# Expert 31's up product in two halves around expert 30's turning products, ahead of its down product

## The reference

```
y = lax.map(expert_block, (x_rows, block_expert))      # per block: its rows, its expert
def expert_block(args):
    xb, e = args
    return (jax.nn.silu(xb @ w1[e]) * (xb @ w3[e])) @ w2[e]
out = jnp.zeros((N, C), F32).at[row_tok].add(y.astype(F32) * row_gate[:, None])
```

## Time and profile before

| | us |
|---|---|
| median of 3 runs | 2261.11 |
| lowest and highest of them | 2261.01, 2263.4 |
| span of the profiled execution, from its first instruction to its last | 2258.9 |
| what lies between that span and the median | 2.2 |
| experts of the first layer in the trace | about 706 to 1199 |
| experts of the second layer in the trace | about 1740 to 2227 |

### The profile page before, as it was taken

How to read it: one execution, slowest core, us unless ns; L and a number is a source line. 1 busy time by engine, 2 the same in 40 slices (tenths; PEclk the granted TensorE clock), 3 DMA queues, 4 the chain that set the end, 5 groups by cost and what they waited for, 6 DMA issues and landing times.

```text
span 2258.9 us, 34449 instructions
## 1 busy us (share of the span) xinstructions
PE 1941.9 (86%) x14540; PEld 1055.0 (47%) x14540; DVE 863.9 (38%) x1608; ACT 454.8 (20%) x1103; POOL 193.1 (9%) x234
## 2 busy tenths in 40 slices
PE   6999788899997888787876999999998888887773
PEld 5843787756744333233333445546845333333321
DVE  6655766674463111101113565761465111110113
ACT  2042666411211000000002005611112000000001
POOL 1000221110001111111110000000000111111110
PEclk9999999999998999999998999999998999999997
DMA  4310001312248999999993222024245999999995
GB/s 151 100 50 0 13 5 61 113 47 102 78 195 309 411 409 405 407 403 415 406 410 134 75 75 75 8 87 149 78 186 222 401 412 408 413 412 409 405 410 199
DMA packets 92146, 510.90 MB, mean 226 GB/s; under 512 B 21824, under 2 KB 22984, under 8 KB 67184
## 3 DMA queue, kind: packets, MB, share of 16 engines
q1 hardware_dynamic: 80896, 492.15, 55.6%
q0 software_dynamic: 10880, 16.81, 2.2%
q10 hardware_dynamic: 240, 0.07, 0.0%
HBM read 503.73 MB, written 24.12 MB: 234 GB/s over the span
## 4 chain that ended last, share of the span: by engine, by line
PE 69%; DMA 17%; DVE 8%; ACT 3%; issue 3%; SPq 0%; ACTq 0%; POOLq 0%; DVEq 0%
DMA big<-in_moe_w 16%; PE ps L2607 15%; PE ps L2063 13%; PE ps L2059 9%; PE ps L2638 7%; PE ps L2042 2%; PE ps L2140 2%; PE ps L2255 2%; PE ps L2408 1%; PE ps L2506 1%; PE ps L2188 1%; PE ps L2518 1%; PE ps L2029 1%; PE ps L2369 1%; PE ps L2414 1%
## 5 line engine op out<-in xcount | busy, mean ns | idle before, releaser
L2607 PE MATMUL ps<-big 128*64 128x512 f32 x2048 | 467.2, 610 | 40.3 <-DMA big<-in_moe_w 37.1
L2607 PEld LDWEIGHTS ps<-big 128*64 128x64 f32 x2048 | 155.9, 140 | 301.6 <-issue 290.5
L2063 PE MATMUL ps<-big 128*128 128x512 f32 x672 | 289.7, 592 | 0.0
L2638 PE MATMUL ps<-big 128*64 128x512 f32 x1024 | 255.9, 646 | 32.6 <-ACT big L1177 32.6
L1916 DVE SCALAR_TENSOR_TENSOR big<-big,ps 128x256 f32<-128x256 f32 x64 | 27.0, 421 | 487.8 <-ACT big L1170 487.8
L2059 PE MATMUL ps<-big 128*128 128x256 f32 x896 | 196.5, 382 | 6.3 <-DVE big L1400 6.3
L2063 PEld LDWEIGHTS ps<-big 128*128 128x128 f32 x672 | 127.4, 190 | 159.0 <-issue 158.7
L1907 DVE TENSOR_TENSOR big<-ps,gain_ffn 128x512 f32<-128x512 f32 x66 | 45.6, 691 | 373.1 <-PE ps L2644 373.1
L2059 PEld LDWEIGHTS ps<-big 128*128 128x128 f32 x896 | 171.8, 192 | 30.3 <-issue 6.5
L2638 PEld LDWEIGHTS ps<-big 128*64 128x64 f32 x1024 | 73.8, 146 | 167.1 <-issue 139.8
L1170 ACT ACTIVATE big<-ps 128x256 f32<-128x256 f32 x64 | 24.6, 384 | 533.1 <-PE ps L2607 533.1
(11 more groups left out here) (351 smaller groups left out, 2442.6 us busy)
## 6 DMA issues: line engine op xcount, KB each, us to landing
big<-in_moe_w SPq DMA_DIRECT2D x182, 2048.0 KB, 31.6
big<-in_rw_wrkv SPq DMA_DIRECT2D x12, 1024.0 KB, 5.1
big<-in_mx_wkv SPq DMA_DIRECT2D x12, 1024.0 KB, 5.0
big<-in_moe_w SPq DMA_DIRECT2D x12, 1024.0 KB, 35.7
big<-in_mb_wqkv SPq DMA_DIRECT2D x12, 1024.0 KB, 6.6
big<-in_mx_wq SPq DMA_DIRECT2D x8, 1024.0 KB, 6.4
big<-in_mx_wo SPq DMA_DIRECT2D x8, 1024.0 KB, 5.0
big<-in_moe_w SPq DMA_DIRECT2D x16, 512.0 KB, 6.9
```

The lines of the kernel that those rows point to most:

```text
L2063: ins = mm(d[:], lhsT=acts[:, k, i * P:(i + 1) * P], rhs=quarter(w)[:, k], start=k == 0, stop=k == 3)
L2607: ins = mm(ps[2 + b][half * BR:(half + 1) * BR, :], lhsT=hgT[b][:, k], rhs=w13[set_][:, :, k, half * 256:(half + 1) * 256], start=k == 0, ...
L2638: ins = mm(ps[5 + b][half * BR:(half + 1) * BR, :], lhsT=hT[b][:, f * BR:(f + 1) * BR], rhs=w2[set_][:, f, half * HB:(half + 1) * HB], sta ...
```

## The change

The last expert's `up` (block 31) is cut into two halves by k. In the step of block 30, PE now does the first half of `up` 31, `turn_act` 30, the second half of `up` 31, `rows_in` for block 32, and `down` 30. The wait for the gathered rows of block 32, which stood in the middle of `down`, is also made ahead of `rows_in`. The diff:

```
 def up(b, set_, number, turn, ks):

+    last = isinstance(number, int) and number == E - 1
     if 0 in ks:
         pe.wait_ge(rowsT_out[l], number + 1)
         pe.wait_ge(act_ready[l], number - 1 + PRE)
-        last = isinstance(number, int) and number == E - 1
...
     ahead = (1 - b, set_1, number + 1, turn_1)
+    if isinstance(number, int) and number in (E - 3, E - 2):
+        up(*ahead, range(0, KT // 2))
+        turn_act(b, number)
+        up(*ahead, range(KT // 2, KT))
+        pe.wait_ge(gathered[l][b], (i * (UNROLL // 2) + (u // 2 + 1)) * 16 + 16)
+        rows_in(b)
+        down(b, set_, number, turn, i * (UNROLL // 2) + (u // 2 + 1))
+        continue
     with runs(number):
         turn_act(b, number)
         down(b, set_, number, turn, i * (UNROLL // 2) + (u // 2 + 1))
     with runs(number + 1):
         rows_in(b)
         up(*ahead, range(KT))
```

## The result

The changed kernel took 2271.19 us (median of 6 runs, 2266.36 to 2276.72), the kernel before 2262.82 beside it (6 runs, 2261.01 to 2266.38). The ratio is 1.0036, with a 95% interval from 1.0023 to 1.0049: slower by 0.36%. In us that is 8.4 more, with 5.2 to 11.1 for the interval. The profiled execution of the changed kernel has a span of 2265.2 and a time of 2267.02, 1.8 more than its span. The old profile's span was 2258.9.

What follows compares the result with a forecast made beforehand. The prediction took TensorE (86% busy) and its hand-overs to bound the changed steps. Order and landings +3.2 and clock falls +2.7 made 5.9 us on 2261.11, hence 2267.0, range 2263.6 to 2269.8.

Steps and rivals of the forecast that it cites:

- both mechanisms: In block 30's step: PE waits for block 31's late weights, and ACT's unchanged order delays block 31's tanh.
- (a): First half of up 31 waits 3.0 us for its second weight piece (3.1 in first layer), holding ready work behind it.
- (b): Second half of up 31 waits for the fourth weight piece, 0.66 us in the second layer, 0.76 in the first.
- (d): Tanh of 31 stands behind block 30's y copy, which waits for down 30; turning products 2.34 us later, second layer.
- The sum of order and landings: Block 31's turning products later by 2.34 us in the second layer and 0.86 in the first: +3.2 us.
- (e): TensorE's clock falls in half of two thin stretches per changed step, costing 1.7 and about 1.0: +2.7 us.
- R3: Rival: the clock falls in all four thin stretches, 8.6 us slower, 2269.7 us; chance 0.14.
- R1: Rival: block 31's pieces land in time, PE never waits, 1.3 us earlier in each layer, 2258.5 us; chance 0.08.
- R4: Rival: nothing measurable moves, as the next layer's start or last loads hide the one changed step, 2261; chance 0.05.

Runs made afterwards that it cites:

- e1: Changed kernel and kernel before, each loading only a quarter of block 30's w2 so block 31's weights land sooner: 2261.43 and 2264.27 us.
- e6: Changed kernel with block 31's tanh before block 30's y copy, and halves of up 31 and down 30 alternating after turning products and rows_in: 2256.53 us, ratio 0.9982.
- e4: The changed kernel timed again without edits, against the kernel before: 2266.23 us, ratio 1.0026.
- e2: Changed kernel with ACT's tanh of block 31 moved ahead of its copy of y of block 30: 2262.24 us, ratio 0.9996.
- e3: Changed kernel with seven products of zeros ahead of up 31's first half and five ahead of block 31's turning products: 2267.95 us, ratio 1.0024.
- run 87: Not a run's label but a count: the unchanged kernel before was run 87 times in four sets, 2255.0 to 2270.1 us.
- e7: Changed kernel with the hardware loop one round shorter and six more steps written out, so block 29 is changed too: 2271.04 us, ratio 1.0050.
- e9: e6 with three products of zeros ahead of block 30's turning products: 2255.96 us, ratio 0.9968.

## Why the prediction was wrong, point by point

The direction, the place and both mechanisms held; the measured 2271.19 lay outside the range of 2263.6 to 2269.8. Of the 4.2 by which it missed 2267.0, 1.7 is the base: the sum started from 2261.11, the median of three runs, and six runs of the same kernel gave 2262.82. The other 2.5 is the difference of the two kernels, 8.4 for a forecast 5.9, and 5.9 lies inside its interval of 5.2 to 11.1.

- **(a), the wait for the second piece.** Forecast 3.0 and 3.1 of idle; the trace has 3.37 and 3.09, other executions of the same kernel 2.95, 2.68, 3.12 and 3.09. e1 shows that it is the landing: with the piece about 4 us sooner, the wait is gone and so is the loss. Right. The Trainium skill, page "DMA: Bandwidth & Descriptors", section "Rules for kernel authors", says to wait on a transfer's semaphore late. These runs agree: the change moved that wait ahead of ready work, waited 3.37, and was 0.25% to 0.36% slower; e6 puts ready work ahead of it, waits 0.50, and is 0.18% faster, with the tanh moved as well.
- **(b), the fourth piece.** Forecast 0.66 and 0.76 of waiting; 0.81 and 0.88 in e4, where the clock didn't fall. Right. Where the clock fell behind the first wait, this wait is gone, so it absorbs 0.8 of the fall.
- **(d), the tanh behind the copy of y.** The idle piece is 2.11 or 2.12 in every trace of the changed kernel. e2 removes it, alone and with nothing else in the step. Right.
- **The sum of order and landings.** Forecast 2.34 in the second layer and a clean 2.56 in the first. Clean, for the second layer and the first, e4 shows 2.3 and 2.5, and e3 2.9 and 2.7 with an overrun of about 0.2 each. Right in size.
- **(e), the clock.** This term was mis-sized. I took a fall in half of the new stretches and 1.0 net for one behind the wait, +2.7 in all. In three traces of the changed kernel it fell behind 4 of 6 waits and in 4 of 6 last `down` products, and one fall behind a wait cost 2.72 and not 1.70. Net of the 0.8 that the second wait absorbs, the three traces give 4.5 / 6 = 0.75 a layer for the first, and 6.4 / 6 = 1.06 for the second, so 3.6 over both layers for the forecast 2.7. From this, against an old kernel that lost 1.5 to falls on average in these steps (12 of 56, four stretches, 1.7 each), the forecast would have been 4.9 + 3.6 - 1.5 = 7.0 rather than 5.9. That explains 1.1 of the 2.5; the rest isn't explained by rows. Three traces can't fix the size either, and e3, with no falls at all, is no faster beyond doubt. R3, a fall in all four, happened in none of the three traces.
- **The base and the range.** This is the step that failed, more than (e). The range was built of the chances of the clock in four stretches, on a median of three runs that lay within 2.4 us. The kernel before, run 87 times in four sets, spreads from 2255.0 to 2270.1 with a standard deviation of 3.3, and so does the changed one (30 runs, 2261.3 to 2276.7, 3.2). The mean difference over all of these is +5.9, give or take 1.4, and the changed kernel's median over its 30 runs is 2267.9, which was inside the range. That these two agree so closely with 5.9 and 2267.0 is partly luck, since the clock term was uncertain by more than that. The first median of six was high, by the draw or by the chip, and the range had no term for either. Much of the scatter isn't made in these two steps: in the 13 traces, the first `up` of the first layer, ahead of everything that the runs changed, already starts anywhere from 704.98 to 710.66. The clock is part of it. Over the 81 runs of the kernel before that have their granted clock on record, a run is about 1.0 us longer for each 0.001 of mean clock less, which takes up about a quarter of the variance. What makes the rest I haven't settled.
- **R1** (pieces there in time) is refuted for this kernel. e1 makes it true: its steps of 21.3 and 21.7 are 1.4 and 1.0 under the clean 22.7, for the 1.3 that R1 gave. **R4** (no effect outside) is refuted by three measurements.
- Only one step per layer was changed, as read from the listing; by e7, the loss would have been larger with two.

## What to carry to other kernels

Before moving a product ahead, look up when its operands land, not only when the engine is idle: filling a bubble of 1.5 us with work whose weights come 3 us later turns the bubble into a longer one, with ready work queued behind it. Then follow the other engines' unchanged orders, since here the same move hid a gate on paper while ScalarE had it behind a copy that waits for the very product meant to cover it. Put ready work ahead of each wait, piece by piece as the data comes; and take the scatter of single runs into a range when the effect is as small as the scatter.

## What the runs showed of the hardware

A fall of TensorE's clock can cost more than the 1.7 us of the forecast: behind a wait of 3.37, half an `up` took 6.37 instead of 3.65, with the granted clock at 0.55 and 0.50 in two stretches in a row. The old trace already had one that cost 2.25, in the first `up` of the first layer:

```profile
707.83 9.34 PE L2607 MATMUL ps<-big 128*64 128x512 f32 x32 [0.78 <-DVE big L1907]
```

In e7, half an `up` took 6.59 behind 8.22 of waiting in the second layer, and 5.32 behind 8.24 in the first. Behind a wait of 2.95, in e4, there was no fall at all; this window lies inside the wait, with 0.00 of PE busy and the clock at 1.00:

```profile
2208.80:2211.70 2.90, 0.00 (x0) 0.01 (x1) 1.01 (x2) 0.38 (x1) 0.00 (x0) 1.00 0.93 390
```

So a wait's length alone doesn't tell; the forecast can only give it a chance.

With products of zeros in the idle time the clock stayed at its upper level in these steps in both layers of e3 and e9: every half of `up` took 3.63 or 3.65, and the last `down` 3.65.
